# A column modulation computed in two halves with the first attention group's chunks between them, and a second gate kept as rows

## The reference

```python
mod = silu(c) @ w_ada + b_ada                 # w_ada is 2048 x 12288, c is one row
shift1, scale1, gate1, shift2, scale2, gate2 = split(mod, 6)
h = rms_norm(x, norm1_w) * (1 + scale1) + shift1
proj = h @ w_in                                # 2048 x 7168: aq ak av (1024 each), gq gf gi gg
... rope, dilated attention, hgrn2 ...
x = x + gate1 * (concat(attn, hg) @ w_out)
h2 = rms_norm(x, norm2_w) * (1 + scale2) + shift2
x = x + gate2 * (square(relu(h2 @ w_ff1)) @ w_ff2)
# second block: h = rms_norm_2(x, g); qkv, stick-breaking attention, w_o, a second squared-relu MLP
```

## Time and profile before

| | |
|---|---|
| median of three runs | 2480.05 us |
| the profiled execution's own time | 2479.47 us |
| its span | 2477.7 us |
| PE matmul busy | 2330.2 us (94%) |
| DVE busy | 1603.8 us (65%) |
| ACT busy | 1037.0 us (42%) |
| POOL busy | 67.0 us (3%) |
| DMA | 519.15 MB, mean 210 GB/s |

### The profile page before, as it was taken

How to read it: one execution, slowest core, us unless ns; L and a number is a source line. 1 busy time by engine, 2 the same in 40 slices (tenths; PEclk the granted TensorE clock), 3 DMA queues, 4 the chain that set the end, 5 groups by cost and what they waited for, 6 DMA issues and landing times.

```text
span 2477.7 us, 27782 instructions
## 1 busy us (share of the span) xinstructions
PE 2330.2 (94%) x10802; PEld 1938.8 (78%) x10802; DVE 1603.8 (65%) x1277; ACT 1037.0 (42%) x878; POOL 67.0 (3%) x63
## 2 busy tenths in 40 slices
PE   0399999998999999999998999999999999999999
PEld 0377888786888888888886888878888888888887
DVE  7789989766566666665557555555655555555554
ACT  1164553433433333333333466565443343433432
POOL 0010000000000000000003000000000000000000
PEclk9999999998999999999999999999999999999999
DMA  7798997743566667565553654534555555555552
GB/s 295 329 370 325 333 328 264 248 159 119 197 234 233 235 237 239 202 196 189 190 186 119 204 164 159 168 128 156 182 189 189 193 187 186 188 185 193 195 186 102
DMA packets 230883, 519.15 MB, mean 210 GB/s; under 512 B 9689, under 2 KB 10146, under 8 KB 224162
## 3 DMA queue, kind: packets, MB, share of 16 engines
q1 hardware_dynamic: 230818, 518.27, 61.2%
HBM read 516.14 MB, written 2.10 MB: 209 GB/s over the span
## 4 chain that ended last, share of the span: by engine, by line
PE 83%; DVE 9%; issue 2%; ACT 2%; DMA 2%; DVEq 1%; POOL 1%; ACTq 1%; SPq 0%
PE PS L237 26%; PE PS L239 26%; PE PS L238 26%; DVE ada_acc L989 2%; DVE w_lo L227 2%; DVE MS L949 2%; PE PS L1467 2%; DMA ada_raw<-in_w_ada_dram 1%; PE PS L1506 1%; POOL rstd L524 1%; PE PS L276 1%; ACT w_hi L223 1%; DVE rt L853 0%; ACTq L314 0%; PE PS L1450 0%
## 5 line engine op out<-in xcount | busy, mean ns | idle before, releaser
L227 DVE TENSOR_TENSOR w_lo<-raw,w_hi 128x2048 fp32r<-128x2048 f32 x392 | 897.8, 2292 | 705.6 <-ACT w_hi L223 700.1
L223 ACT ACTIVATE w_hi<-raw 128x2048 fp32r<-128x2048 f32 x392 | 750.9, 1916 | 1128.2 <-PE PS L239 1128.2
L237 PE MATMUL PS<-w_hi,A_hi 128*128 128x512 f32 x2112 | 834.4, 395 | 9.9 <-DVE A_lo L329 5.2
L239 PE MATMUL PS<-w_hi,A_lo 128*128 128x512 f32 x2112 | 824.4, 390 | 0.0
L238 PE MATMUL PS<-w_lo,A_hi 128*128 128x512 f32 x2112 | 824.0, 390 | 0.0
L237 PEld LDWEIGHTS PS<-w_hi,A_hi 128*128 128x128 f32 x2112 | 398.2, 189 | 91.6 <-issue 7.5
L239 PEld LDWEIGHTS PS<-w_hi,A_lo 128*128 128x128 f32 x2112 | 397.6, 188 | 83.9
L238 PEld LDWEIGHTS PS<-w_lo,A_hi 128*128 128x128 f32 x2112 | 398.2, 189 | 80.4 <-issue 0.5
L237 PE MATMUL PS<-w_hi,H_hi 128*128 128x512 f32 x1024 | 402.3, 393 | 0.1
L239 PE MATMUL PS<-w_hi,H_lo 128*128 128x512 f32 x1024 | 399.0, 390 | 0.0
L238 PE MATMUL PS<-w_lo,H_hi 128*128 128x512 f32 x1024 | 398.5, 389 | 0.0
(11 more groups left out here) (260 smaller groups left out, 1140.3 us busy)
## 6 DMA issues: line engine op xcount, KB each, us to landing
raw<-in_w_ff_dram SPq DMA_DIRECT2D x128, 1024.0 KB, 5.1
raw<-in_mlp_w_in_dram SPq DMA_DIRECT2D x64, 1024.0 KB, 5.5
raw<-in_mlp_w_out_dram SPq DMA_DIRECT2D x64, 1024.0 KB, 4.9
raw<-in_w_in_dram SPq DMA_DIRECT2D x56, 1024.0 KB, 7.9
X<-in_w_ada_dram SPq DMA_DIRECT2D x96, 512.0 KB, 5.9
raw<-in_sb_w_qkv_dram SPq DMA_DIRECT2D x48, 1024.0 KB, 5.1
ada_raw<-in_w_ada_dram SPq DMA_DIRECT2D x32, 1024.0 KB, 7.2
raw<-in_w_out_dram SPq DMA_DIRECT2D x16, 1024.0 KB, 5.0
```

Of the source, the lines that this page charges most:

```text
L223: act.activation(w_hi[:, j, :, :], raw[:, j, :, :], ACT.Copy).then_inc(hi_rdy, 1)
L227: dve.tensor_tensor(w_lo[:, j, :, :], raw[:, j, :, :], w_hi[:, j, :, :].bitcast(F32), ALU.subtract).then_inc(lo_rdy, 1)
L237: pe.matmul(bank(pair + t), h, w_hi[:, j, k, :], start=first, stop=False)
L239: mm = pe.matmul(bank(pair + t), l, w_hi[:, j, k, :], start=False, stop=last)
```

## The change

1. The opening of DVE: the masks that need only POOL's constants come first, and the work for rope and the hgrn2 bounds moves in between the fifth and the sixth piece. x is fetched before the two broadcasts.
2. A piece is now 128 rows by the same 1024 columns of both sections, so after 16 pieces shift1 and scale1 are known for one half of the columns. DVE takes 14 of the 16; the last two PE sums by itself, with the piece as weights and silu(c) as the one column (`piece_sums`). There are three sets of 16 one-column matmuls a half, in PE's order: piece 14, `MS`, piece 15.
3. The twelve chunks of group 0 run in another order: for the first half of the rows q, k, v (6 chunks, `HEAD`), then for the second half (6 chunks). The loads of the first eight stand between the pieces in SP's order, their low parts between the pieces in DVE's.
4. With both q and k finished later in the group, their squares, norms, turns and copies move (`at_steps`). The ring pieces start at slot 7, two a slot, where 18 stood in slots 0 to 11 before; so they end at slot 60, where they ended at 56.
5. In the first MLP gate2 is summed by PE with ones against the accumulated rows (`gate_rows`, after units 10 and 12), and DVE adds the bias, one more transfer of 1 MB, into `gate_w` (`gates`). DVE multiplies `ACC` by it and adds it to `X` already in the last unit but one, and the last unit's product goes from PSUM through one multiplication and one addition into `X`. POOL's four pairs, ACT's four copies, the diagonals and the columns are gone. The loop of the MLP is cut into three on PE and DVE.

The diff, without renamed semaphores, moved masks and the same edits repeated on another engine:

```diff
@@ -75,6 +75,14 @@
...
+AT0_ORDER = [(b, k) for h in range(2) for b in range(3) for k in (2 * h, 2 * h + 1)]
+HEAD = CH * 3 // 2
+ADA_PE = 2
+ADA_DVE = KT - ADA_PE
+LOADS_AFTER = {(0, 9): 0, (0, 11): 1, (0, 13): 2, (1, 0): 3, (1, 2): 4, (1, 4): 5, (1, 6): 6, (1, 9): 7}
+LOW_AFTER = {(0, 11): 0, (0, 13): 1, (1, 1): 2, (1, 3): 3, (1, 5): 4, (1, 7): 5, (1, 9): 6, (1, 11): 7}
...
@@ -82,7 +90,7 @@
 def ada_pieces(slot):
 
     def before(x):
-        return 3 * x // 2 if x <= CH * 3 else 3 * CH * 3 // 2 + 2 * (x - CH * 3) - sum(v < x for r in LEVEL_SLOTS for v in r)
+        return max(0, 2 * (x - HEAD - 1)) - sum(v < x for r in LEVEL_SLOTS for v in r)
...
                     sp.wait_ge(lo_rdy, 4 * (B - 1) + j + 1)
...
 
...
+            def load_at0(n):
+                b, k = AT0_ORDER[n]
+                load(n // CH, n % CH, w_in[:, k, :, w_cols_at0[b]:w_cols_at0[b] + NC_])
+
+            ada = a["w_ada"].rearrange("a (k p) (s n) -> p (a k) s n", p=P, n=D)
+            for h in range(2):
+                for k in range(KT):
+                    r = KT * h + k - CH
+                    if r >= 0 and r % KT < ADA_DVE:
+                        sp.wait_ge(ada_used, ADA_DVE * (r // KT) + r % KT + 1)
+                    elif r >= 0:
+                        sp.wait_ge(ada_pe, ADA_PE * (r // KT) + r % KT - ADA_DVE + 1)
+                    sp.dma_start(ada_raw[:, k % CH, :].rearrange("p (s n) -> p s n", s=2),
+                                 ada[:, k, 0:2, D // 2 * h:D // 2 * (h + 1)]).then_inc(ada_in[k % CH], 16)
...
+                    if (h, k) in LOADS_AFTER:
+                        load_at0(LOADS_AFTER[h, k])
+            for n in range(len(LOADS_AFTER), CH * 3):
+                load_at0(n)
+
...
+                    sp.wait_ge(gate_w_used, KT - 1)
+                    sp.dma_start(gate_w[:, 0, :], a["b_ada"][0:1, GATE2 * D:(GATE2 + 1) * D].to_broadcast([P, D])).then_inc(gate_w_in[0], 16)
                 with sp.Fori(first, NU - 1) as u:
                     up(M + 1 + 2 * u, u + 1)
                     down(M + 2 + 2 * u, u)
...
-            for b in range(D // NC_):
...
-                pool.tensor_tensor(ACC[:, :, cols], ACC[:, :, cols],
-                                   (SQ, RE)[b // 2][:, b % 2, :].unsqueeze(1).to_broadcast([P, T, NC_]), ALU.mult)
-                pool.drain()
-                pool.tensor_tensor(X[:, :, cols], X[:, :, cols], ACC[:, :, cols], ALU.add).then_inc(x_block, 1)
...
-                normalise(act, X, Y0, c)
+                normalise(act, X, X, c)
+            for n in (0, 1):
+                split_hi(act, 0, n)
             act.wait_ge(g_rdy, 1)
-            turn_act(act, 0, g1, mod[:, SHIFT1, :], GN, between={1: lambda: split_hi(act, 0, 0), 4: lambda: split_hi(act, 0, 1)})
...
+            turn_act(act, 0, g1, mod[:, SHIFT1, :], turned, steps=ALL[:4], banks=FIRST)
+            for n in range(2, CH * 2):
+                split_hi(act, n // CH, n % CH)
+            act.wait_ge(g_rdy, 2)
+            turn_act(act, 0, g1, mod[:, SHIFT1, :], turned, steps=ALL[4:], first=4, banks=SECOND,
+                     between={1: lambda: split_hi(act, 2, 0)})
+            split_hi(act, 2, 1)
             groups = proj_groups()
             for i, (kind, idx, B0, nb) in enumerate(groups):
...
+                for s in range(0 if i else HEAD, CH * nb):
...
-            for b in range(4):
-                gate(4 + b, b, (SQ, RE)[b // 2][:, b % 2, :])
-                if b in (1, 2):
-                    split_hi(act, QKV0, b - 1)
...
+            def half_modulation(h):
...
+                n = KT * (1 + ADA_PE)
+                dve.wait_ge(ada_sum, h + 1)
+                dve.wait_ge(ada_pe, ADA_PE * (h + 1))
+                dve.tensor_reduce(ada_part[:, 0, :], bank(6, n * h, n * h + n).rearrange("p (c m) -> p c m", m=1 + ADA_PE),
+                                  AX_X, ALU.add)
+                d()
+                dve.tensor_tensor(mod[:, SHIFT1:GATE1, kts], ada_part[:, 0, :].rearrange("p (s k) -> p s k", s=2),
+                                  colA[:, 0:2 * KT].rearrange("p (s k) -> p s k", s=2)[:, :, kts], ALU.add).then_inc(mod_rdy, 1)
+                d()
...
+                dve.scalar_tensor_tensor(out=g1[:, kts], in0=mod[:, SCALE1, kts], scalar=1.0,
+                                         in1=colA[:, r0 + kts.start:r0 + kts.stop], op0=ALU.add, op1=ALU.mult).then_inc(g_rdy, 1)
...
             for h in range(2):
-                for k in range(KT):
+                for k in range(ADA_DVE):
...
-                    dve.wait_ge(ada_used, CH + KT * h + k + 1)
+                    if (h, k) == (0, 4):
+                        bounds_and_angles()
+                    if (h, k) == (1, 0):
+                        half_modulation(0)
+                    if (h, k) == (1, 1):
+                        turn_first(ALL[0:2], 0)
+                    if (h, k) == (1, 2):
+                        turn_first(ALL[2:4], 2)
+                    if (h, k) in LOW_AFTER:
+                        n = LOW_AFTER[h, k]
+                        split_lo(dve, n // CH, n % CH)
+                    dve.wait_ge(ada_used, ADA_DVE * h + k + 1)
...
+                    dve.wait_ge(gate_w_in[0], 16 * (KT // 2 + 1))
+                    for b in (2 * n, 2 * n + 1):
+                        dve.wait_ge(gate_mm, 4 + b + 1)
+                        cols = slice(NC_ * b, NC_ * (b + 1))
+                        dve.tensor_tensor(gate_w[:, 1, cols], bank(6 + b % 2), gate_w[:, 0, cols], ALU.add).then_inc(gate_rdy, 1)
+
+                def down(B, U, par, pair=None, into=None):
...
+                        if into is not None:
+                            cols = slice(NC_ * j, NC_ * (j + 1))
+                            d()
+                            dve.tensor_tensor(ac, ac, gate_w[:, 1, cols].unsqueeze(1).to_broadcast([P, T, NC_]), ALU.mult)
+                            d()
+                            dve.tensor_tensor(into[:, :, cols], into[:, :, cols], ac, ALU.add)
...
-                    for n in range(ADA_EARLY, ADA_BLOCKS):
-                        ada_collect(n, ada_acc[:, (n - ADA_EARLY) // 2, n % 2, :])
-                with dve.Fori(turns, NU // 2 - 1) as i:
+                if m == 0:
+                    for n, (i0, i1) in enumerate(((turns, 5), (5, 6))):
+                        with dve.Fori(i0, i1) as i:
+                            for e in range(2):
+                                up(M + 3 + 4 * i + 2 * e, 2 + 2 * i + e)
+                                down(M + 4 + 4 * i + 2 * e, 1 + 2 * i + e, e)
+                        gates(n)
...
-                        down(M + 4 + 4 * i + 2 * e, NU * m + 1 + 2 * i + e, e)
+                        up(M + 3 + 4 * i + 2 * e, 2 + 2 * i + e)
+                        down(M + 4 + 4 * i + 2 * e, 1 + 2 * i + e, e, into=X if e else None)
...
-            dve.wait_ge(mod_mm, 3)
-            modulation(GATE2, GATE2 + 1)
-            d()
-            gate_block(4, 0, GATE2, DG[:, 0, :])
...
-                dve.tensor_tensor(ACC[:, :, cols], ACC[:, :, cols], PS[:, pb:pb + 2, :], ALU.add).then_inc(acc_read, 1)
+                dve.tensor_tensor((SQ, RE)[b % 2][:, :, :], PS[:, pb:pb + 2, :], gate_w[:, 1, cols].unsqueeze(1).to_broadcast([P, T, NC_]),
+                                  ALU.mult).then_inc(acc_read, 1)
+                d()
+                dve.tensor_tensor(X[:, :, cols], X[:, :, cols], (SQ, RE)[b % 2][:, :, :], ALU.add).then_inc(x_done, 1)
...
+            def half_sums(h, m, column):
+
+                for c in range(KT):
+                    at = (1 + ADA_PE) * (KT * h + c) + m
+                    lhs, rhs = column(c)
+                    mm = pe.matmul(bank(6, at, at + 1), lhs, rhs, start=True, stop=True)
+                return mm
+
+            def piece_sums(h, m):
+
+                k = ADA_DVE + m
+                pe.wait_ge(ada_in[k % CH], 16 * (h * (KT // CH) + k // CH + 1))
+                half_sums(h, 1 + m, lambda c: (ada_raw[:, k % CH, P * c:P * c + P], sc[:, k:k + 1])).then_inc(ada_pe, 1)
+
+            def sums(h):
+
+                piece_sums(h, 0)
+                pe.wait_ge(ada_used, ADA_DVE * (h + 1))
+                half_sums(h, 0, lambda c: (MS[:, h, P * c:P * c + P], ones[:, 0:1])).then_inc(ada_sum, 1)
+                piece_sums(h, 1)
...
-            pe.wait_ge(mod_rdy, 1)
-            turn(0, Y0)
+            turn(0, X, steps=ALL[:4], banks=FIRST)
+            pe.wait_ge(ada_used, 1)
+            sums(0)
+            for n in range(HEAD):
+                at0_chunk(pe, n)
+            pe.wait_ge(y_rdy, 4)
+            turn(0, X, steps=ALL[4:5], first=4, banks=SECOND)
+            sums(1)
+            pe.wait_ge(mod_rdy, 2)
+            turn(0, X, steps=ALL[5:6], first=5, banks=SECOND[1:])
+            for i, b in ((6, 7), (7, 6)):
+                pe.wait_ge(a_hi, i - 1)
+                turn(0, X, steps=ALL[i:i + 1], first=i, banks=(b,))
...
-                        if gates:
```

(66 more changed lines are left out.)

229 lines of the change are left out of this document (109 added, 120 removed).

## The result

The changed kernel takes 2491.55 us (median of 5 runs, 2489.8 to 2495.11) against 2480.05 before: the ratio is 1.0049 (95% interval 1.0037 to 1.0061). It is slower by 11.5 us, where 20 us less was forecast. The profiled span is 2489.2 us against 2477.7, also 11.5 apart, so the two traces can be laid side by side.

| stretch on PE, from one instruction to the next | before | after | difference | forecast |
|---|---|---|---|---|
| start to the turn of k in group 0 | 191.86 | 202.69 | +10.8 | -13.9 |
| to the second gate spread of the out projection | 332.31 | 331.60 | -0.7 | 0 |
| to the last turn of `MIX` | 36.53 | 45.46 | +8.9 | +1.5 |
| to the turn of unit 15 of the first MLP | 734.85 | 738.31 | +3.5 | +3.2 |
| to the fourth turn of x | 61.25 | 50.80 | -10.4 | -10.2 |

The account below looks back on a forecast made before the run. It took PE to be bound by its late start, waiting 92.2 us for DVE's sums. 2479.47 less 13.9 (opening), plus 1.5 (ring pieces), less 7.0 (MLP's end) gave 2460.1, stated as 2460, range 2456 to 2464.

Parts of the forecast that it names:

- The sums of PE: Opening: PE makes three sets of 16 sums in a row per half, at 3.5 us a set (6.99 for 32).
- First half: Opening, first half of the columns: pieces land at 65.1, 67.6 and 70.1, and its modulation is done at 76.3.
- Second half: Opening, second half of the columns: DVE works 51.7 us to 128.0, DMA's 45 is hidden, seventh chunk starts at 140.0.
- Rival C: PE's sums are short: 16 take 1.6 us instead of 3.5, saving 4 in each half; 2452 us, chance 0.20.
- The seventh chunk's clock: Group 0, after PE idles about 20 us: part of the chunk runs at 1.2 GHz, costing 2 us, between 0 and 5.4.
- The turn of k: Group 0: PE waits 2.6 us for the norm chain; the turn starts at 178.0 against 191.86, 13.9 saved.
- Ring pieces: Slots 57 to 60, beside the levels: eight pieces moved out of the opening lose 1.5 us, between 0 and 10.7.
- rival B: Out projection: the ring pieces are not hidden and cost 10.7 us instead of 1.5; 2469 us, chance 0.10.
- End of the first MLP: Turn of unit 15 to fourth turn of x: 51 us, 10.2 saved, 2.6 and 0.6 against it; 7.0 saved net.
- A: Opening: DMA ends the second half at 359 GB/s, 2.9 us a transfer, seventh chunk at 143.7; 2464 us, chance 0.13.
- D: Opening: DMA runs at 266 GB/s, 3.9 us a transfer, so the chunk starts at 180; 2500 us, chance 0.04.
- E: Opening: the six chunks don't fit ahead of the second sums, up to 32.6 us return; 2493 us, chance 0.03.

## Why the prediction was wrong, point by point

**What bounds the kernel.** Right: PE has no slack behind the opening. What an experiment takes out of one stretch of PE comes out of the time, within some 2 us: 16.5 at the turn of k became 14.5, 7.0 in the out projection became 6.1, and 10.4 at the MLP's end, less 3.5 for the gate matmuls, became 7.6.

**The sums of PE: the step that failed.** The prediction took 6.99 us for 32 matmuls as two sets of 16, "three sets of 16 sums in a row at 3.5 us". It was one set. Two things in the trace said so: that row waits 32.21 us, while the other wait of the pair in the earlier trace rows is 60.0, so there must be an earlier set of the same kind; and the window 60 to 80 holds another 6.96 us of PE in x32, which the prediction never asked about. The written order gave x32 for both sections together, the trace x32 for one. So the term that was mis-sized is the set: 6.83 us measured, 3.5 taken. Term by term, the trace against the forecast:

- First half: three sets 20.6 instead of 10.5, +10.1. Piece 14 came at 68.3 instead of 65.1, +3.2 (a transfer cost 2.7 and not 2.5: the window 30 to 68, shown below, has 383 GB/s at a share of 1.01).
- From the first modulation to DVE's last piece: 51.7 forecast; 89.8 to 140.9 in the trace, -0.6.
- Second half: piece 14 landed 2.2 before DVE's end, and its set held PE until 145.5. From DVE's end to the last sum 18.4 instead of 7.0, +11.4. Of these 4.6 are the rest of piece 14's set, which the forecast had as over by then, and 6.8 the two sets behind it.
- From there to the seventh chunk 5.0, as forecast, and 38.35 on to the turn of k against 38.0.

That is 24 us of the error of 24.7, and 21.5 of them stand in the two rows of sets. No rival doubted the number upward, though the step from 14 to 16 pieces on DVE costs only 4.8 and would have been the first thing to compare: at the right price the sets on PE lose even on paper (13.7 against 4.8 a half).

**Rival C and the clock.** C doubted the same number, but downward: PE would just have worked. It didn't take place, and the granted clock shows what the sets of the second half ran at (window, columns as in the earlier trace rows; the second row is the first half's first chunk):

```profile
138.66:159.30 20.64, 20.64 (x96) 20.55 (x96) 2.24 (x1) 0.00 (x0) 0.00 (x0) 0.50 0.61 234
...
93.92:99.60 5.68, 5.68 (x13) 4.46 (x14) 1.41 (x1) 5.54 (x7) 0.00 (x0) 1.00 1.03 396
```

PE made chunks at full clock up to 131.5, stood idle for 6.54 us, and then made all three sets at 0.50, the level of 1.2 GHz. For the first half the reading says 1.00, but it says so too for the chunk behind it, whose matmuls start 0.43 us apart instead of 0.23; so it can't be relied on there. No run has a set that is known to have run at 2.4 GHz. The nearest row is that of four narrow f32 matmuls (16 columns, weights of 128 x 128) among the chunks of the kernel before, at a granted clock of 1.00:

```profile
1307.36 0.96 PE L1459 MATMUL PS<-ada_part,SEL 128*128 128x16 f32 x8
1308.17 0.47 PE L237 MATMUL PS<-w_hi,H_hi 128*128 128x512 f32 x1
```

They take 0.81 us, 0.20 a matmul, against 0.43 in the sets. So a set at full clock would cost some 3.2 us (an estimate from this row), near the forecast's 3.5 and twice C's 1.6: C took its price from turns, which leave one record a matmul where these leave two.

**The seventh chunk's clock.** Right. It took 7.3 us for 5.44 (window, columns as in the earlier trace rows), 1.9 more where 2 was taken; a whole chunk at 1.2 GHz would have been 5.4 more. The second row is the stretch of DMA named above:

```profile
164.34:171.66 7.32, 7.32 (x26) 5.91 (x25) 4.63 (x5) 5.86 (x8) 0.00 (x0) 0.74 0.78 266
...
30.00:68.00 38.00, 0.00 (x0) 0.00 (x0) 32.83 (x32) 3.82 (x2) 0.00 (x0) 1.00 1.01 383
```

The mean granted clock in the chunk is 0.74, between the two levels: it is 0.51 up to 168.25 and 1.00 from there on, so only part of it was slow. The Trainium skill (TensorE: Matmul & The Clock Gate, Part 1) says that an idle engine falls back to 1.2 GHz. The trace agrees: after the idle 6.54 us the granted clock is 0.50. It stays there through 20.6 us of sets, in which PE is not idle.

**The turn of k.** The wait is 2.74 where 2.6 was taken.

**Ring pieces.** Wrong, and rival B came nearer in size, not in cause. "The later reload of x (slot 60) has ten slots to land" asked when x is needed; it had to ask what is queued behind the wait for it. The pieces and section sums on DVE cost 1.9, near the 1.5; the rest, 7.0, was a weight load behind a wait in SP's order. The prediction's own list of steps had the queue of the MLP's bias checked in just this way, and not this one.

**End of the first MLP.** Right in its terms: 51 us from the turn of unit 15 to the fourth turn of x, and 50.80 measured. PE's waits in it are 1.3 and 0.2 before chunks of the last units, where 2 was taken, and 1.35 for `A_lo`, where 1.9 was. The list puts the 1.3 down to no engine, and its cause was not tested. A pair of gate matmuls costs 1.77, two of them 3.5, against 0.6 + 2.6.

**Rivals A, D and E.** A and D had the second half wait for DMA. Once the first half's modulation was made, DVE never waited for one of its pieces and PE's wait of 6.54 for piece 14 ended before DVE had finished, so neither took place. E did not either: the sixth chunk ended 7 us ahead of the sums. The time of 2491.55 is near E's 2493 by chance.

## What to carry to other kernels

Before a duration from a trace is divided by a count, compare that count with the calls in the code, and look for all rows of the line, not only the one on the path; a group whose price carries the sum is worth one view of its own. When work is shared out to an idle engine, set its price there against the price where it was: an idle engine is no gain if the new work stands behind the last input, and its price is the one at the clock that the engine will have there. And where a transfer is moved to wait longer, price not only when its data is needed but every transfer that is written behind it in the same queue.

## What the runs showed of the hardware

- A set of 16 one-column f32 matmuls, 32 records, costs 6.83 us. It does so at a granted clock of 0.50 (138.66 to 159.30), and also in the first half (68.34 to 89.0), where the reading of 1.00 is doubtful, as said above. Each record comes 0.21 us after the last. Four f32 matmuls of 16 columns at a granted clock of 1.00 leave 8 records 0.10 us apart. That the weight load is what is paid with so few columns is argued from the windows, where PEld is as busy as PE (20.55 and 20.64 us), and was not tried.
- The same sum with 128 x 128 ones against 512 columns (the gate rows) took 0.59 us a record; a pair of blocks cost PE 1.77 us.
